# v of an attention pair formed by token in 384-column matmuls, with its near part passed through memory, in place of three feature-wise units and their transposes

## The reference, cut to what matters

```
hn = rms_norm(h, norm_w)
proj = hn @ w_in
u_f, g_f, q, k, v, g_a = split(proj)
...
q = rms_norm(q per head) * 64 ** -0.5;  k = rms_norm(k per head)
for c, (window, dilation) in enumerate(((128, 1), (512, 4), (2048, 16))):
    o_c, lse_c = dilated_window_attention(q[c], k[c], v[c], window, dilation, slopes)
o = softmax over the three configurations of lse, times o_c, summed
y_a = o * silu(g_a)
h = h + concat(y_f, y_a) @ w_out
```

## Time and profile before

| | us |
|---|---|
| median of 3 runs (1458.49 to 1459.30) | 1458.94 |
| the profiled execution | 1458.79 |
| its span, first to last instruction | 1457.0 |
| PE busy | 1450.7 |
| POOL busy | 957.9 |
| DVE busy | 854.6 |
| ACT busy | 518.1 |

### The profile page before, as it was taken

The page is one execution under the profiler, slowest core; times in us unless marked ns, Lnnn a source line. Parts: engine busy times, 40 slices in busy tenths (PEclk is TensorE's granted clock), DMA queues, the critical chain, the costliest instruction groups (busy, mean ns, idle before and its releaser), DMA issues.

```text
span 1457.0 us, 22805 instructions
## 1 busy us (share of the span) xinstructions
PE 1450.7 (100%) x8006; PEld 1196.1 (82%) x8006; DVE 854.6 (59%) x1217; ACT 518.1 (36%) x929; POOL 957.9 (66%) x945
## 2 busy tenths in 40 slices
PE   9999999999999999999999999999999999999999
PEld 7788888888888888888988888888898888888887
DVE  3577787867877858433755555500248583846733
ACT  5481541371263211112522222200253554636441
POOL 5456766765775799888277777799426664655554
PEclk9999999999999999999999999999999999999999
DMA  9344433532633345535023223334223221222232
GB/s 378 131 117 131 145 103 120 197 116 71 223 124 113 116 145 173 131 104 200 25 92 101 89 99 101 101 122 142 83 98 116 84 77 60 85 72 72 73 129 73
DMA packets 68125, 172.29 MB, mean 118 GB/s; under 512 B 7744, under 2 KB 24512, under 8 KB 66656
## 3 DMA queue, kind: packets, MB, share of 16 engines
q1 hardware_dynamic: 45648, 150.57, 31.6%
q10 hardware_dynamic: 22416, 20.92, 4.6%
HBM read 167.20 MB, written 4.27 MB: 118 GB/s over the span
## 4 chain that ended last, share of the span: by engine, by line
PE 97%; DVE 1%; DMA 1%; ACT 0%; SPq 0%; issue 0%; DVEq 0%; ACTq 0%
PE ps L632 17%; PE ps L635 17%; PE ps L634 17%; PE ps L649 6%; PE ps L651 6%; PE ps L650 6%; PE ps L1009 4%; PE ps L1008 4%; PE ps L1007 4%; PE ps L908 1%; PE ps L1030 1%; PE ps L1034 1%; PE ps L1032 1%; PE ps L1204 1%; PE ps L1283 1%; PE ps L1284 1%
## 5 line engine op out<-in xcount | busy, mean ns | idle before, releaser
L582 POOL TENSOR_SCALAR w_hi<-raw 128x512 fp32r<-128x512 f32 x386 | 261.9, 697 | 465.1 <-PE ps L635 220.7
L587 POOL TENSOR_TENSOR w_lo<-raw,w_hi 128x512 fp32r<-128x512 f32 x386 | 530.6, 1396 | 0.0
L632 PE MATMUL ps<-h_hi,w_hi 128*128 128x512 f32 x880 | 344.7, 392 | 0.0
L635 PE MATMUL ps<-h_hi,w_lo 128*128 128x512 f32 x880 | 342.7, 389 | 0.0
L634 PE MATMUL ps<-h_lo,w_hi 128*128 128x512 f32 x880 | 342.5, 389 | 0.0
L632 PEld LDWEIGHTS ps<-h_hi,w_hi 128*128 128x128 f32 x880 | 165.2, 188 | 35.4 <-issue 1.9
L635 PEld LDWEIGHTS ps<-h_hi,w_lo 128*128 128x128 f32 x880 | 165.2, 188 | 34.8
L634 PEld LDWEIGHTS ps<-h_lo,w_hi 128*128 128x128 f32 x880 | 165.3, 188 | 33.9
L649 PE MATMUL ps<-h_hi,w_hi 128*128 128x512 f32 x352 | 140.2, 398 | 0.4 <-ACT qsq_hi L1708 0.4
L651 PE MATMUL ps<-h_hi,w_lo 128*128 128x512 f32 x352 | 137.4, 390 | 0.0
L650 PE MATMUL ps<-h_lo,w_hi 128*128 128x512 f32 x352 | 137.3, 390 | 0.0
(11 more groups left out here) (450 smaller groups left out, 2857.2 us busy)
## 6 DMA issues: line engine op xcount, KB each, us to landing
raw<-stream SPq DMA_DIRECT2D x231, 512.0 KB, 3.4
ada_raw<-ada SPq DMA_DIRECT2D x64, 256.0 KB, 3.9
abc<-acs_dram ACTq DMA_DIRECT2D x16, 512.0 KB, 6.9
ada<-ada_first SPq DMA_DIRECT2D x4, 1024.0 KB, 12.4
ada_pair<-ada_first SPq DMA_DIRECT2D x4, 1024.0 KB, 20.5
raw<-stream SPq DMA_DIRECT2D x8, 256.0 KB, 14.5
xr<-x_classes ACTq DMA_DIRECT2D x1, 2048.0 KB, 9.3
x_dram<-xr ACTq DMA_DIRECT2D x1, 2048.0 KB, 7.2
```

The source lines that it names most:

```text
L582: nc.gpsimd.tensor_scalar(hi[:, w], raw[:, raw_slot, w], 1.0, 1.0, ALU.mult, ALU.mult).then_inc(split_hi, 1)
L587: ins = nc.gpsimd.tensor_tensor(lo[:, w], raw[:, raw_slot, w], hi[:, w].bitcast(F32), ALU.subtract)
L632: nc.tensor.matmul(ps[:, bank], hi[:, w], x_hi[:, k0 + k], start=start and k == 0, stop=False)
L635: mm = nc.tensor.matmul(ps[:, bank], lo[:, w], x_hi[:, k0 + k], start=False, stop=stop and k == tiles - 1)
```

## The change

The three v units of a pair are laid out anew on the host. `V_PLACES` sorts their 24 blocks by depth: unit 6 holds depths 0 and 1 of all three configurations and two blocks of depth 2, unit 7 the third block of depth 2, depths 3 and 4 and one block of depth 5, unit 8 the rest. PE now lets a 128 x 128 block of `h` (128 tokens, one depth) stand in the array and moves the three blocks of weights past it, 384 columns. `V_BLOCKS` says where a depth's three blocks lie over both slots; depth 5 has no such even row of blocks and is done in two pieces, of 128 and 256 columns. There are four token tiles t, each in its own PSUM bank (1, 0, 2, 3). The result is token by feature at once, so the transposes, `vT`, `v_turned` and `v_ready` go.

ACT copies each bank (384 columns) to `vN_next` (`take_v`), writes its near part to memory (`near_dram`, one DMA) and at the end of the pair fetches it from there in another token order with three DMAs (`move_v`) in place of two of the three copies. The weighted sum of the next pair waits for these (`v_moved`, 49 a pair).

The diff, cut to what matters:

```diff
+V_BANKS, V_ENDS = (1, 0, 2, 3), (2, 3, 1, 0)
...
-                if 7 <= j <= 9:
-                    c = j - 7
-                    pe.wait_ge(evacuated, E_ATT + N_ATT * p + 6 + c + 1)
...
-                    for t in range(NT):
-                        mm = nc.tensor.transpose(ps[:, 7, t * P:(t + 1) * P], vT[:, t * P:(t + 1) * P], ident)
-                    mm.then_inc(v_turned, 1)
+            def v_product(t, k, start=False):
+
+                q = slice(t * P, (t + 1) * P)
+                pieces = (((3, 4, 1), 0), ((8, 10, 1), P)) if k == 5 else ((V_BLOCKS[k], 0),)
+                for h, w in ((h_hi, v_hi), (h_hi, v_lo), (h_lo, v_hi)):
+                    for (first, end, step), at_ in pieces:
+                        moved = w[:, first:end:step]
+                        mm = nc.tensor.matmul(ps[:, V_BANKS[t], at_:at_ + (end - first + step - 1) // step * P],
+                                              h[:, k, q], moved, start=start, stop=(k == KT - 1), skip_group_check=True)
+                    start = False
+                return mm
+
+            def v_first(p, a):
+
+                u = U_ATT + N_ATT * p + 6
+                pe.wait_ge(split_done, u + 1)
+                for t in range(NT):
+                    if t < 2:
+                        pe.wait_ge(evacuated, E_ATT + N_ATT * p + 5 + t)
+                    elif is_first(p):
+                        pe.wait_ge(wf_ready, 1)
+                    else:
+                        pe.wait_ge(biased, 1 + 8 * a + 4 + t - 1)
+                    v_product(t, 0, start=True)
+                    v_product(t, 1)
+                    if is_first(p) and t == 0:
+                        follow(p, 5)
+                pe.wait_ge(split_done, u + 2)
+                for t in range(NT):
+                    mm = v_product(t, 2)
+                mm.then_inc(units_done, 1)
+                follow(p, 6)
+                for t in range(NT):
+                    v_product(t, 3)
+                    v_product(t, 4)
+
+            def v_last(p):
+
+                pe.wait_ge(split_done, U_ATT + N_ATT * p + 9)
+                for t in V_ENDS:
+                    mm = v_product(t, 5)
+                mm.then_inc(units_done, 1)
+                for t in V_ENDS:
+                    v_product(t, 6)
+                    v_product(t, 7).then_inc(v_formed if t != V_ENDS[-1] else units_done, 1)
...
             for x in range(8, 2 * N_ATT):
+                if x == 12:
+                    v_first(0, None)
+                    v_last(0)
+                if 12 <= x < 18:
+                    continue
                 half(0, x)
...
-                    half(a + 1, 6 * r)
...
+                    if r == 2:
+                        v_first(a + 1, a)
...
                     turn_p(a, r, 1)
...
+                    if r == 2:
+                        v_last(a + 1)
...
+                    copied = A(vN_next[:, :, t], ps[:, V_BANKS[t], 0:CFG * P].rearrange("p (c w) -> p c w", c=CFG),
+                               ACT.Copy)
...
+                act.dma_start(near_dram.rearrange("(i r) w -> i r w", r=NT), vN_next[:, 0]).then_inc(near_stored, 16)
...
-                A(vN[:, 1:], vN_next[:], ACT.Copy).then_inc(v_moved, 1)
...
+                A(vN[:, 2:], vN_next[:, 1:], ACT.Copy).then_inc(v_moved, 1)
+                act.wait_ge(near_stored, 16 * (p + 1))
+                quarters = near_dram.rearrange("(t x) w -> x t w", t=NT)
+                act.dma_start(vN[:, 1], quarters).then_inc(v_moved, 16)
...
```

More of the change, by code:

```diff
@@ L273, in build @@
         qrt = g("qrt", [P, 3, S])
-        vT = g("vT", [P, S])
         ufT = g("ufT", [P, S])
@@ L291, in build @@
         gg_dram = nc.dram_tensor("gg_dram", (2, D), F32, kind="Internal").ap()
+        near_dram = nc.dram_tensor("near_dram", (S, P), F32, kind="Internal").ap()
         x2_dram = nc.dram_tensor("x2_dram", (P, NT, D), F32, kind="Internal").ap()
@@ L401, in build @@
         qk_moved = sem("qk_moved")
-        v_turned = sem("v_turned")
-        v_ready = sem("v_ready")
+        v_formed = sem("v_formed")
+        near_stored = sem("near_stored")
         v_moved = sem("v_moved")
@@ L1211, in attend @@
                     pe.wait_ge(biased, 1 + 8 * a + 2 * (r + 1))
+                if r == 2 and not isinstance(a, int):
+                    pe.wait_ge(evacuated, E_ATT + N_ATT * (a + 1) + 7)
                 if r == 0:
-                    pe.wait_ge(v_moved, 3 * (a + 1))
+                    pe.wait_ge(v_moved, V_MOVED * (a + 1))
                     pe.wait_ge(ya_steps, 1 + 2 * a)
@@ L1252, in _ @@
                         token_transform(a)
-                    half(a + 1, 6 * r)
-                    half(a + 1, 6 * r + 1)
-                    half(a + 1, 6 * r + 2)
-                    half(a + 1, 6 * r + 3)
+                    if r == 2:
+                        v_first(a + 1, a)
+                    else:
+                        for x in range(4):
+                            half(a + 1, 6 * r + x)
                     turn_p(a, r, 0)
@@ L1708, in take @@
                     A(qsq_hi[:], bank, ACT.Square).then_inc(evacuated, 1)
[L1709 to L1715, removed]
                 elif j == 9:
@@ L1727, in take, with take_sum @@
                     A(sga_next[:], bank, ACT.Silu).then_inc(evacuated, 1)
-                if 1 <= j <= 6:
-                    m = j - 1
+                if 1 <= j <= 5:
+                    take_sum(p, j - 1)
+            def take_sum(p, m):
                     act.wait_ge(qk_total, 6 * p + m + 1)
-                    if not (first and m < 3):
+                    if not (is_first(p) and m < 3):
                         act.wait_ge(qk_steps, 12 * p + 2 * (m - 3) + 2)
@@ L1735, in take, with take_v @@
                       scale=1.0 if m < 3 else 1.0 / HP).then_inc(qk_root, 1)
[L1736 to L1741, removed]
+            def take_v(p):
+                for n, t in enumerate(V_ENDS):
+                    if n == 0 and not is_first(p):
+                        act.wait_ge(near_stored, 16 * p)
+                        act.wait_ge(v_moved, V_MOVED * p)
+                    if n < NT - 1:
+                        act.wait_ge(v_formed, 3 * p + n + 1)
+                    else:
+                        act.wait_ge(units_done, 1 + U_ATT + N_ATT * p + 9)
+                    copied = A(vN_next[:, :, t], ps[:, V_BANKS[t], 0:CFG * P].rearrange("p (c w) -> p c w", c=CFG),
+                               ACT.Copy)
+                    if n:
+                        copied.then_inc(evacuated, 1)
+                act.wait_ge(evacuated, E_ATT + N_ATT * p + 9)
+                act.dma_start(near_dram.rearrange("(i r) w -> i r w", r=NT), vN_next[:, 0]).then_inc(near_stored, 16)
             def take_heads(p):
@@ L1751, in move_v @@
             def move_v(p):
-                act.wait_ge(v_ready, 3 * p + 3)
+                act.wait_ge(evacuated, E_ATT + N_ATT * p + 9)
                 if not is_first(p):
                     act.wait_ge(attended, 1 + 5 * p)
-                A(vN[:, 1:], vN_next[:], ACT.Copy).then_inc(v_moved, 1)
-                A(vN[0:64, 0, 0:NT - 1], vN_next[0:64, 0, 1:NT], ACT.Copy).then_inc(v_moved, 1)
-                A(vN[64:P, 0, 1:NT], vN_next[64:P, 0, 0:NT - 1], ACT.Copy).then_inc(v_moved, 1)
+                A(vN[:, 2:], vN_next[:, 1:], ACT.Copy).then_inc(v_moved, 1)
+                act.wait_ge(near_stored, 16 * (p + 1))
+                quarters = near_dram.rearrange("(t x) w -> x t w", t=NT)
+                act.dma_start(vN[:, 1], quarters).then_inc(v_moved, 16)
+                act.dma_start(vN[0:64, 0, 0:NT - 1], quarters[0:64, 1:NT]).then_inc(v_moved, 16)
+                act.dma_start(vN[64:P, 0, 1:NT], quarters[64:P, 0:NT - 1]).then_inc(v_moved, 16)
             def exp(a, r, h):
@@ L1788, in _ @@
             for j in range(N_ATT):
-                take(0, j)
+                if j == 6:
+                    take_sum(0, 5)
+                    take_v(0)
+                if not 6 <= j < 9:
+                    take(0, j)
                 if j == 4:
@@ L1806, in _ @@
                         take_odd(a)
-                    take(a + 1, 3 * r)
+                    if r == 2:
+                        take_sum(a + 1, 5)
+                    else:
+                        take(a + 1, 3 * r)
                     pt_out(a, r, 0)
@@ L1812, in _ @@
                         A(wf_now[:], blocks(wf, a + 1), ACT.Copy).then_inc(wf_ready, 1)
-                    take(a + 1, 3 * r + 1)
+                    if r != 2:
+                        take(a + 1, 3 * r + 1)
                     pt_out(a, r, 1)
@@ L1816, in _ @@
                         take_heads(a + 1)
-                    take(a + 1, 3 * r + 2)
+                    if r == 2:
+                        take_v(a + 1)
+                    else:
+                        take(a + 1, 3 * r + 2)
                 hi_attention(a)
@@ L2506, in lay_out @@
     for i2 in range(4):
-        for m in (q, k, v):
+        for m in (q, k):
```

(2 more changed lines are left out.)

16 lines of the change are left out of this document (10 added, 6 removed).

## The result

Median of six runs 1465.90 us (1465.06 to 1467.20) against 1458.82 us (1458.49 to 1459.30) of the kernel before, six runs as well: a ratio of 1.0049, 95% interval 1.0039 to 1.0060. The change makes the kernel 7.1 us slower; the forecast was 6.9.

The account below looks back on a forecast made before the run. PE was taken to bound the kernel. Products -1.3, bias waits +4.5 and pair 0's waits +3.75 gave +6.95 us on 1458.79: 1465.7 us. Its own range was 1462.5 to 1468.5; 8 in 10, 1461.0 to 1472.0.

Parts of the forecast that it names:

- The steps of 384, 256 and 128 columns: PE's v matmuls: 0.1735 us for 384 columns, 0.120 for 256, 0.110 for 128.
- The prediction's 0.3 us a pair and 1.2 in all by that formula: PE's v products: by the skill page's gap formula, 0.3 us less a pair and a total some 1.2 us lower.
- dear short pieces: Rival, depth 5 on PE: 128-column pieces cost a 512-column step, 5.6 us more in all, 1471.3 us; chance 0.20.
- dear blocks: Rival, v products: a 384-column step costs as much as one of 512, 18 us more, 1483.7 us; chance 0.03.
- The products, -0.33 a pair: v on PE: new steps cost 0.99 us more, dropped transposes save 1.32; -0.33 a pair, -1.3 in four.
- The wait for the bias, +1.5 in each of three pairs: Pairs 1 to 3: tile 2's bank holds scores until DVE's `add_bias` has read them, so PE waits; +4.5 us.
- After a wait PE needs 0.14 us to start: PE after any wait: 0.14 us to start, with the longer first step 0.22 us in all.
- the 1.2 to 1.5 that the prediction named as its sign: List of PE's waits, changed profile: three waits of 1.2 to 1.5 us for DVE's bias line would confirm the forecast.
- the rival without waits: Rival: banks are free in time, leaving only -1.3 us of PE work, 1457.5 us; chance 0.12.
- Pair 0, +3.75 and -0.33, so +3.42: Pair 0: PE waits 2.05 us for unit 5's copy, 1.40 for `wf_ready`, 0.3 for unit 9's split; products -0.33.
- Memory, nothing: Near part's DMAs out and back: covered by other work, counted as nothing; one over 20 us would be paid in full.
- ACT is no bound and I count nothing for it: ACT in each pair: six copies become four of 384 columns, priced at nothing.

Follow-up runs that it names:

- run 4: Kernel before the change, with only one of the four transposes of each v unit left in place: 1455.33 us, ratio 0.9974.
- run 7: Changed kernel with a third depth of tiles 0 and 1 before the bias wait, and free banks for pair 0's tiles: 1458.85 us, ratio 0.9999.
- Run 1: Changed kernel with depths 0 to 2 of tiles 0 and 1, 18 matmuls not 12, before PE's bias wait: 1463.33 us, ratio 1.0035.
- run 3: Changed kernel with eight and five filler matmuls into a spare bank at pair 0's two waits, which stay: 1466.85 us, ratio 1.0057.
- run 5: Changed kernel with ACT's two residual (`x_res`) loads issued one step later, after the first class of pair 3: 1465.11 us, ratio 1.0048.

## Why the prediction held, point by point

- **The steps of 384, 256 and 128 columns.** Forecast 0.1735 and, for a pair of short pieces, 0.23. Measured 0.174; in pair 0's timeline of the changed kernel the pairs of short pieces start at 1118.37, 1118.61 and 1118.83, 0.23 apart. The Trainium skill ("TensorE: Matmul & The Clock Gate", "Back-to-back issue gap") gives 0.163 at 384 columns by its formula for isolated matmuls; the trace does not agree, its steps are 0.173 to 0.174. The prediction's 0.3 us a pair and 1.2 in all by that formula keep 0.110 for the 128-column pieces, and come to 0.25 and 1.0. The rivals of dear short pieces and dear blocks fall.
- **The products, -0.33 a pair.** Pairs 1 to 3 lose 0.94 to 1.03 where the wait costs 1.31: -0.28 to -0.37. With run 4 for the transposes this term stands, though run 7 shows that two waits met just in time take most of it in pairs 1 to 3.
- **The wait for the bias, +1.5 in each of three pairs.** It is there, at the place and for the instruction named, with 1.31. DVE came when forecast, 3.36 us after the first v matmul (1186.78 to 1190.14; 1181.83 to 1185.19 in the earlier trace rows). Two sizes were off. The twelve steps ahead took 2.20 us (1186.78 to 1188.98) and not 2.08, as the first of them is 0.27 long. And "After a wait PE needs 0.14 us to start" is too much: it was 0.05 behind DVE (1190.14 to 1190.19) and 0.06 behind ACT in pair 0 (1104.58 + 0.60 to 1105.24), so the 0.14 of the earlier trace rows is not the rule here, and why it is longer there is open. +4.5 became +3.9. The list of waits counts from the modelled end of the matmul before (1188.81 + 0.34) and leaves out the longer first step; it has 1.0 each, under the 1.2 to 1.5 that the prediction named as its sign, and 1.1 for `wf`, under its 1.2 to 2. Run 1 took the wait out and 3.1 came back by the marks; the rival without waits falls with it.
- **Pair 0, +3.75 and -0.33, so +3.42.** At full clock it is 3.07 with unit 9's split in time and 3.47 with it late by 0.4, as in the profiled run; the forecast had 0.3 for that. PE started again at 1105.24 and 1107.62; the forecast's 1105.42 and 1107.86 count in 0.08 for the longer first step, so 1105.34 and 1107.78 compare with these.
- **Memory, nothing.** No wait on PE names `vN`. The DMAs (KB each, us from issue to landing) took 4.2 us out and 2.9 and 4.5 back:

```profile
near_dram<-vN_next ACTq DMA_DIRECT2D x4, 256.0 KB, 4.2
vN<-near_dram ACTq DMA_DIRECT2D x4, 256.0 KB, 2.9
vN<-near_dram ACTq DMA_DIRECT2D x8, 96.0 KB, 4.5
```

- **Two steps failed.** "ACT is no bound and I count nothing for it" priced ACT's copies and left out its DMA issues and what stands behind them in its queue in the output stage: a wait of 0.3 us in the profiled run, 1.6 in run 3. And the sum takes every step at full clock; in the profiled run it fell after the two new gaps in PE's work, and that cost 1.5 us.

The sum was 6.9 and the profiled execution has 8.4: the three pairs came 0.5 lower (3.0 against 3.5), the clock is 1.5 more, the output stage 0.4 more, and pair 0 otherwise as forecast. The prediction's own lower end, 1462.5, is mis-summed: by its terms, 1.2 less for the steps and a third less of the 7.95 of waits, it comes to 1461.9. The median lies nearer to the forecast because four of the six runs had no fall. So the forecast was right for its main reason, the waits, and part of the closeness is errors that cancel.

## What to carry to other kernels

A new layout of a product is worth its steps only if its destination is free when its first matmul comes: here the new steps and the missing transposes together were worth 1.3 us, and the PSUM banks chosen for the tiles cost over five times as much in waits. Before giving a tile a bank, read when the bank's last reader ends and how many steps stand ahead of it in PE's queue; a depth more for the free tiles in pairs 1 to 3 and other banks in pair 0 together took the whole loss away. And price a DMA on a compute engine's queue by its issue, and by what then starts late behind it.

## What was not expected of the hardware

- After waits of 1.7 and 1.1 us on PE, with 1.1 us of matmuls between them, the granted clock fell to 0.50 for some 3.4 us in the profiled run, and a 384-column step took 0.32 us. Waits of 1.7 and 1.0 in the profiles of runs 1 and 5 brought no fall.
- A wait that is met within hundredths of a microsecond of PE's arrival still made the first step behind it 0.28 us in place of 0.174 (run 7); one that was met 0.6 us before PE came to it did not (the changed kernel, tile 3).
- Issuing one DMA of 96 to 256 KB held ACT's queue for 0.33 to 0.69 us in the changed kernel, and two of 1024 KB together for 1.25 and, in run 3, 1.72 us.
- Two DVE instructions took 0.76 and 0.69 us where they ran ahead of POOL's split (run 5), and 1.61 and 1.67 where they ran beside it (the changed kernel).
